# Gate and second-value projections moved beside the expert gathers, projections in tile pairs

## The reference

```
n = rmsnorm(h, norm_mix_g);  proj = n @ w_in
u, vm, o_pre, i_pre, f_pre, qs, ks, vs = split(proj)     # 512 512 512 4 4 512 512 512
c  = silu(conv4(u) + conv_b)                              # depthwise, 4 taps, along time
ym = mLSTM(c, vm, sigmoid(o_pre), i_pre, f_pre)           # 4 heads of 128, chunked state
ys = stick_breaking_attention(qs, ks, vs)                 # 8 heads of 64, causal
h  = h + concat(ym, ys) @ w_out
n  = rmsnorm(h, norm_ffn_g)
q  = n @ w_query                                          # 8 heads, 2 halves of 128
s  = q . sub_keys; top 16 of each half; top 16 of the 256 sums -> 16 experts a head
act = gelu(n . expert_u[eidx]);  h = h + sum_k softmax_k * act_k * expert_v[eidx]
out = rmsnorm(h[lead:], norm_final_g)
```

## Time and profile before

| | us |
|---|---|
| median of 3 runs | 3559.83 |
| lowest and highest run | 3544.12, 3566.91 |
| span of the profiled execution, first to last instruction | 3523.4 |
| PE busy (matmul), share of the span | 2191.2 (62%) |
| DVE busy | 2181.0 (62%) |
| POOL busy | 1939.1 (55%) |
| ACT busy | 628.4 (18%) |
| moved by DMA in the whole | 1156.71 MB, of which 1073.87 MB by the indirect gathers |

### The profile page before, as it was taken

The page is one execution under the profiler, slowest core; times in us unless marked ns, Lnnn a source line. Parts: engine busy times, 40 slices in busy tenths (PEclk is TensorE's granted clock), DMA queues, the critical chain, the costliest instruction groups (busy, mean ns, idle before and its releaser), DMA issues.

```text
span 3523.4 us, 32706 instructions
## 1 busy us (share of the span) xinstructions
PE 2191.2 (62%) x10776; PEld 1123.3 (32%) x10776; DVE 2181.0 (62%) x5516; ACT 628.4 (18%) x1358; POOL 1939.1 (55%) x2079
## 2 busy tenths in 40 slices
PE   8999986455665456545775457646774577534433
PEld 6767762122322223212321233213421343211100
DVE  4544357665766675666666576667765666655753
ACT  1221132110211012111221032102311232101000
POOL 0000026666666665666666665666666656666665
PEclk9999997676777677766777687767887688776656
DMA  5211369999999999999999999999999999999998
GB/s 194 67 35 44 114 233 356 376 388 366 350 365 384 379 354 347 374 390 351 361 363 384 366 361 356 382 373 369 379 364 378 362 335 367 365 356 378 366 368 331
DMA packets 337952, 1156.71 MB, mean 328 GB/s; under 512 B 36404, under 2 KB 50424, under 8 KB 336760
## 3 DMA queue, kind: packets, MB, share of 16 engines
q0 software_dynamic: 294912, 1073.87, 80.2%
q1 hardware_dynamic: 42872, 80.75, 6.6%
HBM read 1136.64 MB, written 17.84 MB: 328 GB/s over the span
## 4 chain that ended last, share of the span: by engine, by line
PE 26%; POOL 20%; issue 16%; DVE 16%; another core or an unknown queue 14%; DMA 5%; ACT 2%; DVEq 0%; POOLq 0%; ACTq 0%
POOL work L705 10%; PE xs L1516 10%; POOL work L688 10%; DVE work L1398 7%; PE xs_ahead L1516 7%; PE acc L1516 6%; DMA work<-expert_u,chosen 4%; PE bank L1516 3%; DVE work L1024 1%; DVE cand L1016 1%; DMA work<-expert_v,idx_v 1%; DVE work L1016 1%; DVE rest L1298 1%; DVE sri L1307 1%
## 5 line engine op out<-in xcount | busy, mean ns | idle before, releaser
L1398 DVE CUSTOM_DVE_ANT_0 work<-work,xs 128x1024 f32<-128x1024 f32 x1003 | 1207.9, 1217 | 511.1 <-DMA work<-expert_u,chosen 322.6
L688 POOL DMA_INDIRECT work<-expert_u,chosen x1024 | 966.9, 944 | 856.1 <-DVE chosen L1024 469.6
L705 POOL DMA_INDIRECT work<-expert_v,idx_v x1024 | 967.3, 945 | 711.2 <-remote 292.8
L1516 PE MATMUL acc<-work,lw 128*32 128x512 f32 x4096 | 819.8, 857 | 579.2 <-DMA work<-expert_v,idx_v 279.6
L1516 PEld LDWEIGHTS acc<-work,lw 128*32 128x32 f32 x4096 | 148.5, 137 | 1017.7 <-issue 565.5
L1516 PE MATMUL bank<-weights,n2T 128*128 128x256 f32 x1024 | 254.0, 403 | 0.0
L1516 PE MATMUL bank<-which_eight,c_spread 128*128 128x16 f32 x128 | 34.5, 348 | 332.7 <-DVE c_spread L1016 176.4
L1516 PEld LDWEIGHTS bank<-weights,n2T 128*128 128x128 f32 x1024 | 201.4, 202 | 106.6 <-issue 79.6
L1516 PE MATMUL xs<-work,weights 128*128 128x128 f32 x1664 | 195.4, 279 | 0.0
L1516 PE MATMUL xs_ahead<-work,neg_tri 128*128 128x512 f32 (+1 forms) x176 | 129.5, 826 | 105.2 <-DVE work L1024 46.9
L1516 PEld LDWEIGHTS xs<-work,weights 128*128 128x128 f32 x1664 | 191.7, 195 | 1.4 <-issue 1.3
(11 more groups left out here) (203 smaller groups left out, 2412.9 us busy)
## 6 DMA issues: line engine op xcount, KB each, us to landing
work<-kv_dram SPq DMA_DIRECT2D x72, 256.0 KB
work<-expert_u,chosen POOLq DMA_INDIRECT x1024
work<-expert_v,idx_v POOLq DMA_INDIRECT x1024
weights<-w_in SPq DMA_DIRECT2D x6, 2048.0 KB, 17.2
mix_dram<-work SPq DMA_DIRECT2D x8, 1024.0 KB, 4.1
weights<-w_queryT SPq DMA_DIRECT2D x4, 2048.0 KB, 7.8
work<-xT SPq DMA_DIRECT2D x9, 512.0 KB, 7.1
kv_dram<-work SPq DMA_DIRECT2D x9, 512.0 KB, 5.9
```

The costliest lines, as they stand in the source:

```text
L688: pool.indirect_dma_start(out=ring_u[:, s, :], out_offset=None, in_=expert_u, in_offset=bass.IndirectOffsetOnAxis(ap=chosen[:, G % KEPT_HE ...
L705: pool.indirect_dma_start(out=ring_v[:, e % RING_V, :], out_offset=None, in_=expert_v, in_offset=bass.IndirectOffsetOnAxis(ap=idx_v[:, G % ...
L1398: nc.vector.tensor_tensor_reduce(s, s, rows[:, :, :].rearrange("p a b -> p (a b)"), 1.0, 0.0, ALU.mult, ALU.add, dots[:, d:d + 1]).then_in ...
L1516: return nc.tensor.matmul(out_, lhsT, rhs, start=start, stop=stop, skip_group_check=True)
```

## The change

ORDER and MIXED_AT give way to one list ITEMS for all engines. It is read by each engine from the front, and each does its part of an item. `BEFORE_UNITS` comes first, then 38 units of UNITS_A, each followed by its row of AFTER_UNIT, then four of UNITS_B with eight folds, `scores(0)` and the picks. The other ten units of UNITS_B and 24 folds are hung on slots of the first tile's gathers (slot 0 is the first dot, slots -16 to -1 are ahead of it).

```
+UNITS_A = ([unit((0,), n) for n in ("u", "ks", "v", "vs")] + [unit((1,), n) for n in SECTIONS]
+           + [u for a in (2, 4, 6) for n in ("u", "ks") for u in halves(a, n)]
+           + [unit((LAST,), n) for n in ("u", "ks")]
+           + [u for a in (2, 4, 6) for u in halves(a, "qs")] + [unit((LAST,), "qs")]
+           + [unit((T,), "v") for T in range(2, TILES)])
+AFTER_UNIT = [
+    [("sums_x", 1), ("sums", 0), ("conv", (0,)), ("norm", 1), ("square", 2)],
+    [("sums_x", 2), ("rows", 0), ("silu", (0,)), ("square", 3)],
+    [("sums_x", 3), ("top", 0), ("norm", 2)],
...
+    [("conv", (2, 3)), ("back", 2), ("sums", 3), ("norm", 6), ("square", 7)],
+    [("sums_x", 7), ("mix", (0, 6)), ("silu", (2, 3)), ("cols", 2), ("rows", 3)],
...
+    [("sums_x", 8), ("conv", (4, 5)), ("mix", (14, 19)), ("cols", 3), ("rows", 4)],
+    [("mix", (19, 21)), ("silu", (4, 5)), ("top", 4), ("raw", 5), ("norm", 8)],
+    [("mix", (21, 25)), ("back", 4), ("sums", 5)],
+    [("mix", (25, 29)), ("cols", 4), ("raw", 6), ("rows", 5)],
+    [("conv", (6, 7)), ("mix", (29, 33)), ("top", 5), ("sums", 6)],
+    [("mix", (33, 37)), ("silu", (6, 7)), ("back", 5), ("rows", 6)],
+    [("mix", (37, 72)), ("cols", 5), ("top", 6), ("raw", 7)],
+    [("mix", (72, 75)), ("conv", (8,)), ("back", 6), ("sums", 7)],
+    [("mix", (75, 77)), ("silu", (8,)), ("cols", 6), ("raw", 8), ("rows", 7)],
...
+UNITS_B = [unit((T,), n) for n in ("so", "vs") for T in range(2, TILES)]
+ITEMS = (BEFORE_UNITS + [x for u, after in zip(UNITS_A, AFTER_UNIT) for x in [u] + after]
+         + [UNITS_B[0], ("fold", (0, 4)), UNITS_B[1], ("scores", 0), UNITS_B[2], ("fold", (4, 8)), UNITS_B[3], ("picks", 0)])
+UNIT_SLOTS = dict(zip((-8, 2, 6, 10, 14, 18, 24, 29, 34, 40), [u[1] for u in UNITS_B[4:]]))
+EVAC_SLOTS = {s + 2: u for s, u in UNIT_SLOTS.items()}
+GATE_SLOTS = {s + 6: u for s, u in UNIT_SLOTS.items() if u[1] == "so"}
+FOLD_SLOTS = {s: n for n, s in enumerate(list(range(4, 12)) + list(range(26, 34)) + list(range(48, 56)), 8)}
+U_EARLY, U_FROM, U_LATER = [0, 1, 2, 3], 48, [4, 5, 6, 0, 1, 2, 3]
+V_EARLY, V_FROM, V_LATER = [8, 9, 10, 11, 12, 14, 15], 32, [13, 16, 7, 12, 14, 15, 8, 9, 10, 11]
+LATE_MIX, LATE_SLOTS = 56, 41
+SCORES_AT = {1: -3, 2: 17, 3: 31, 4: 45, 5: 59, 6: 73, 7: 88}
```

A half unit of a pair (tiles a, a + 1) takes 256 of the 512 columns for 256 positions, 16 matmuls of 256 columns (32 in the trace):

```
+                if f is not None:
+                    to = projected(b).rearrange("p (c a t) -> p c a t", c=2, a=2)
+                    for c in range(2):
+                        for k in range(KC):
+                            last = mm(to[:, c, :, :], w_sec[n][:, k, (2 * f + c) * P:(2 * f + c + 1) * P],
+                                      pairs_x[tiles[0]][:, :, k, :], k == 0, k == KC - 1)
```

All nine normalised tiles are kept (eight in rows of the rings, the last in `y[0]`), so the first 48 u gathers have four rows and the first 32 v gathers seven; the rest of the rows come free with the last "vs" unit and its store. All units are now copied out by ACT. SP takes its loads and stores in the order of ITEMS too; a load of x waits behind the stores listed before it:

```
+            for kind, what in ITEMS:
+                if kind == "square" and what >= 2:
+                    load_x(what)
+                if kind == "silu":
+                    store_c(what)
...
+            def store_c(tiles):
+                sp.wait_ge(silu_ready, GROUPS.index(tiles) + 1)
```

More of the change, by code:

```diff
@@ new lines @@
+FOLD_SLOTS = {s: n for n, s in enumerate(list(range(4, 12)) + list(range(26, 34)) + list(range(48, 56)), 8)}
+BANKS = [([u[1] for u in UNITS_A], 2), ([u[1] for u in UNITS_B], 4)]
+ORDINAL = {}
+for _list, _bank in BANKS:
+    for _u in _list:
+        ORDINAL[_u] = 1 + sum(1 for v in ORDINAL if v[1] == _u[1])
+STAGED = [u for l, _ in BANKS for u in l if u[1] in ("v", "so", "vs")]
+GROUPS = [tiles for tiles, n, f in BANKS[0][0] if n == "u" and not f]
+GATE_STEPS = ("raw", "sums", "rows", "back")
@@ L793, in fold, with exp_conv @@
+            def exp_conv(tiles):
+                act.wait_ge(conv_ready, GROUPS.index(tiles) + 1)
+                wait(act, silu_ready, GROUPS.index(tiles))
+                w = len(tiles) * P
+                nc.scalar.activation(sig[:, :, 0:w], conv[:, :, 0:w], ACT.Exp, scale=-1.0).then_inc(conv_exp, 1)
             def fold(a, b):
@@ L1199, in add_parts @@
                 Lm(last)
-                update_state(T)
+                dve.sem_inc(nd_ready, 1)
             def make_h(T):
@@ L1771, in n2_rows, with bank7_free @@
                 last.then_inc(xs_ready, 1)
+            seven = {"scores": 0, "picks": 0, "weights": 0}
+            def bank7_free():
+                wait(pe, scores_free, seven["scores"])
+                wait(pe, idx_v_ready, seven["picks"])
+                wait(pe, lw_ready, seven["weights"])
             def scores(G):
@@ L1849, in mixing @@
+                if n == tail(M, "n2_t"):
                     n2_t(M)
             square_sums(0)
-            for T, n in ORDER:
-                project(T, n)
-                if (T, n) == (1, "qs"):
+            for kind, what in ITEMS:
+                if kind == "sums_x":
+                    if what > 0:
+                        square_sums(what)
+                if kind == "raw":
+                    raw_gates(what)
+                if kind == "sums":
+                    forget_sums(what)
+                if kind == "rows":
+                    turn_rows(what)
+                if kind == "back":
+                    turn_back(what)
+                if kind == "unit":
+                    project(what)
+                if kind == "lead_a":
@@ L1864, in _ @@
+                if kind == "fold":
+                    fold(*what)
+                if kind == "scores":
                     scores(0)
-                if (T, n) == TURN_AT:
+                if kind == "picks":
                     turn_idx(0)
             for T in range(0, LAST + 2):
-                for n in range(0 if T else FIRST_SLOT, slots(T)):
+                for n in range(0 if T else SLOTS + FIRST_SLOT, slots(T)):
+                    at = (T - 1) * SLOTS + n
                     I, o = divmod(T * SLOTS + n, TOPK)
```

862 lines of the change are left out of this document (474 added, 388 removed), and 3 rows, old and new, of the table MIXED_AT.

## The result

The changed kernel takes 3697.41 us (median of 4 runs, 3687.47 to 3713.22), the kernel before 3562.45 (3544.12 to 3566.91) beside it: ratio 1.040, interval 1.036 to 1.044. A second set of runs of the same two kernels gave 3702.86 for 3553.84, 1.043 (1.040 to 1.046). The sign was forecast, the size wasn't: +135 to +149 us for +58, and above the range of 3530 to 3675.

The account below looks back on a forecast made before the run. The prediction held the head bound by PE and the gathers by the DMA engines. Head -90 + 25 + 77 + 14 = +26 us, gathers +32, together +58, about 3615 us, range 3530 to 3675.

Parts of the forecast that it names:

- What leaves the head: PE work ahead of the first gather: 11 units, four folds, cheaper half units and small waits go, -90 us.
- the x tiles: Head: PE waits for square sums of late-loaded tiles 2, 3 and 5, 12.9, 6.3 and 6 us, +25 us.
- DVE in the way of the gate steps: Head: PE waits for short gate steps listed behind DVE's long pair convolution and silu, +77 us (57 to 90).
- The clock: Head: units behind nine PE gaps run slower, 1.6 us for each gap, +14 us (0 to 30).
- Start: First gathers: the 17th comes 65 us behind scores(0), before 54.5, as dots wait for gate products and routing, +10 us.
- The small ring: Gathers until 48: fewer open u and v rows, put-off units can hold back a sum_set, +15 us (0 to 80).
- the store of vs8: Gather 32 of v: POOL waits for this store, and slot 48's fold for a 2 MB load, +7 us (0 to 20).
- Mixing of tile 2 in 41 slots: Beside the gathers: periods of 4 slots, crowding offset by earlier waits that go, 0 us (-10 to +15).
- A: Rival: the head's waits are covered, only the x tiles cost; 3527 us, down to 3500; chance 0.22.
- B: Rival: half of the 77 and little clock loss, head 25 us shorter, the stream eats it; 3560 us; chance 0.2.
- C: Rival: PE at 1.2 GHz beside the gathers, v gathers stand behind its work, 80 us and not 15; 3680; chance 0.13.

Follow-up runs that it names:

- e1_order: The changed kernel with rows 11 to 24 of its list reordered, gate steps ahead of the pairs' convolution and silu: 3600.52 us, 1.0148 of the kernel before.
- e14_changed_busy: The changed kernel with unread matmuls right in front of the nine steps PE waits for, beside the changed kernel on one chip: 3679.55 us, 1.0370.
- e10_all_busy: e5_head_v8 with the scores of head 1 at slot -12 and unread matmuls ahead of six short head waits: 3289.91 us on a quicker chip, 1.0097.
- e7_units_back: e4_head with all 14 units and the folds back ahead of the gathers, full rings, tile 2's mixing still in 41 slots: 3617.39 us, 1.0163.
- e16_mix45: e10_all_busy with head 1's scores at slot -3, 4 u and 10 v early rows, put-off units and last folds moved, mixing in 45 slots: 3555.81 us, 1.0006.
- e5_head_v8: e4_head with eight rows for the early v gathers and three for the early u gathers, for seven and four: 3584.73 us, 1.0077.
- e4_head: The changed kernel with both head edits, gate steps ahead of pair steps and x tiles loaded, squared and summed at other rows: 3581.12 us, 1.0109.

## Why the forecast was wrong, step by step

- **What leaves the head, -90, and the x tiles, +25: right.** PE's work at the full clock fell by 83.5 us, for 86 forecast. The waits for square sums were 13.4, 4.2 and 5.9 us for 12.9, 6.3 and 6.
- **DVE in the way of the gate steps, +77: right**, 78 by the profile, and row for row within 2.1 us. DVE's pair reciprocal took 6.55 us, 6.7 forecast. A wait of 5.11 us behind the tile 1 units wasn't on the list.
- **The clock, +14 (0 to 30): the first failed term.** It was 42 us. I had taken 1.6 us a gap, from a single unit of before, and nine gaps. The units behind the nine long gaps lost 1.1 to 2.6 us each, the four behind the waits for x tiles and for tile 1's gates 0.8 to 2.0, and one behind a wait of 3.30 us lost 1.8. Three units with no wait over 1.3 us right ahead of them lost as much (1.7, 2.1 and 2.4), and small matmuls were slow as well. 24 us of it went with the long gaps (e1_order), 16 with unread matmuls in them (e14_changed_busy); in the reordered head 14 us more went with unread matmuls in six short ones (e10_all_busy).
- **Start, +10: right** (+6.6).
- **The small ring, +15, and the store of vs8, +7: the second failed term**, 43 us. The step that failed is setting PE's work (131 us) against the slots' time (150) as if the two could overlap freely. POOL waits for one `sum_set` at a time, 46.3 us in four such waits, and seven rows leave no room for a unit ahead of it; with the units and the small ring taken away the stretch is 67.9 us and not 110.9 (e7_units_back). The range, 0 to 80, held it; the value I took didn't.
- **Mixing of tile 2 in 41 slots, 0 (-10 to +15): the third failed term**, +33 and +25 in the two traces, 18 in the medians of the pair of kernels that differ in it. I compared a period of 4 with tile 8's 5 and called it crowding without a price, or rather set it off against waits of before that would go. Whether it is the period or the number of slots stays open.
- **The rivals.** A and B spoke of the head being cheaper and are refuted by its waits. C, PE at 1.2 GHz beside the gathers, gave 3680 and was the nearest to the time, but by luck: between 540 and 700 us three units took 8.1 to 9.2 us and seven took 7.03, the clock from 540 to 640 was 0.88, and most of the time was lost in the head and the mixing. (B's sum is slightly off: 25 us shorter and a stream that eats 32 is 3567, not 3560; it changes nothing.)
- **The sum.** In the first trace the 193rd gather is 94 us later than forecast: 39 in the head (28 by the clock, 8 by waits, the unlisted one of 5 among them, 3 by work that didn't leave), 21 in the ring, 33 in the mixing, 5 between them, less 3 at the start. In the medians it is 77 to 91. All three errors have one sign: I priced each new wait well, and at little or nothing what the wait does to what stands behind it.

## What to carry to other kernels

When work is reordered, write down for every engine which short step another engine waits for, and put it ahead of the long ones in the same row; that was 88 us of the first gather's time here, and the ratio went from 1.040 to 1.015, for no change in work. A gap on PE costs itself and, in most cases seen here, 1 to 2.6 us in the unit behind it, so many small gaps are dearer than their sum; unread matmuls right in front of the wait (never ahead of a step that someone else waits for) are a cheap cure and a cheap test. Work put off into another stage is free only if its buffers are too: with a ring of less than two whole sets each set waits for the one before it. That a chain with too few slots per block costs all at once, and not in proportion, is likely by the 18 us of e16_mix45, but not shown.

## What the runs showed of the hardware

Short gaps count, though not each time. In e5_head_v8 a unit behind a wait of 2.86 us took 9.40 us (64 matmuls of 128 columns; 7.39 elsewhere) and one behind 3.30 us took 9.15 (32 of 256; 7.15 elsewhere):

```profile
273.91 1.41 PE L1709 MATMUL acc<-ident,work 4*128 4x4 f32 x6 [2.86 <-issue]
...
276.12 9.40 PE L1709 MATMUL xs<-y,weights 128*128 128x128 f32 x64
...
336.00 1.41 PE L1709 MATMUL acc<-ident,work 4*128 4x4 f32 x6 [3.30 <-issue]
...
337.77 9.15 PE L1709 MATMUL xs<-work,weights 128*128 128x256 f32 x32
```

The same gap needn't cost the same. Behind a wait of 1.86 us for the same step a unit took 9.04 us in this trace and 7.41 in that of e4_head, whose head is the same code; behind the same wait of 5.11 us it was 9.17 and 7.55.

Chips differ. On one the kernel before took 3259.79 us (7 runs) where its medians were 3543 to 3562 on the others; gathers 1001 to 1501 took 680 us there against 740 to 760, while a unit of 32 matmuls took the same 7.15. Absolute times of experiments from different chips can't be set side by side, only their ratios and their traces.
